# Loading the cached values in runs of eight pages instead of one page after each key page

## The chip, the cores and the metric

The kernel runs on one core of one Trainium2 chip. The metric is the device time of one launch in microseconds (us). Three runs of the kernel before took 4829.04, 4834.27 and 4845.87 us, so its median is 4834.27 us.

The core has a matrix engine (PE; its weight loads are listed as PEld), a vector engine (DVE), a scalar engine (ACT), a general engine (POOL) and a queue engine (SP) that here does nothing but wait for semaphores and issue DMA transfers, strictly in the order of its program.

## The reference

One inference step of a decoder with two layers. Each layer projects 2048 prompt tokens and 8 x 4 sample tokens, runs an RWKV-7 recurrence over one half of the width and differential attention over the other, and projects back. The part that this change touches is the attention:

```python
def diff_attend(q, k, v, q_pos, k_pos, lam):
    s = jnp.einsum('bqhcd,bkhcd->bhcqk', q, k) / math.sqrt(DIFF_HEAD_DIM)
    s = jnp.where(k_pos[None, :] <= q_pos[:, None], s, -jnp.inf)
    p = jax.nn.softmax(s, axis=-1)
    attn = p[:, :, 0] - lam * p[:, :, 1]
    return jnp.einsum('bhqk,bkhe->bqhe', attn, v)

def diff_sample(q, k, v, lam, k_pool, v_pool, page_table):
    k_past = k_pool[page_table].reshape(B, -1, DIFF_HEADS, 2, DIFF_HEAD_DIM)
    v_past = v_pool[page_table].reshape(B, -1, DIFF_HEADS, DIFF_V_DIM)
    k_all = jnp.concatenate([k_past, k], axis=1)
    v_all = jnp.concatenate([v_past, v], axis=1)
    return diff_attend(q, k_all, v_all, past + jnp.arange(T), jnp.arange(past + T), lam)
```

The prompt has 4 heads of 2048 positions. Each of the 8 sample sequences has 2048 cached positions, kept in 16 pages of 128 positions (for all 4 heads together a page of keys is 256 KB, and a page of values as well). Where a page lies in HBM is read from the page table at run time.

## The kernel before

A loop runs the two layers. Each layer has five stages with a barrier between them: input projection, RWKV, attention, the RWKV part of the samples, output projection. The change is in the attention stage, `attn_sync` and its helpers, all of it code for the SP queue.

**The prompt's attention.** It goes over tiles t = 0 to 63, sixteen for each of four heads h, each tile being 128 query rows of a head. PE makes the scores of tile t in blocks j of 512 keys (`scores`, L1354), DVE copies them out of PSUM, ACT takes the exponentials (L1158), DVE combines the two maps, PE turns the result of tile t-2 (`turn_map`, L1370), ACT copies it out (L1167) and PE multiplies it with the values (`values`, L1382). Queries and keys of a head, which the code calls its maps, are two transfers of 1 MB each into one of two buffers `kq[h % 2]` (`load_map`, L985). The head's values come by a third transfer of 1 MB (`load_values`, L1006).

**The samples' attention rides along.** The table `BESIDE` lists 200 places (t, j) between blocks of the prompt's work. Sequence b owns 31 of them, and they start at place 24 b; its piece number k is done at place 24 b + k. In `beside_tensor`:

- pieces 1 to 16 turn key pages 0 to 15 with four transposes each (L1118) and then signal `t_made`;
- pieces 9, 11, 14 and 17 make the scores of four pages each (L1110);
- pieces 21 to 24 turn the probabilities (L1127);
- pieces 22, 23, 26 and 27 multiply with value groups 0 to 3, four pages each (L1138), and signal `pv_done`.

A sequence with odd b = 2 h + 1 is turned in tiles 16 h + 9 to 16 h + 13. PE runs its program in order: a transpose that waits for its page holds up everything behind it, the prompt's work too.

**Buffers and what the SP queue waits for.** Key pages go through KS = 4 buffers, so page p of a sequence can be asked for when page p - 4 has been turned (the wait in `keys_sync`). Value pages go through two buffers of four pages. Group n, counted over all sequences (n = 4 b + g), waits until group n - 2 has been multiplied. The maps of head h + 1 wait until head h has begun. All of these are issued by SP, one after the other.

**The order on the SP queue before.** For each sequence b: key page 4, value page 0, key page 5, value page 1, and so on to key page 11 and value page 7; then key pages 12 to 15. For odd b below 7 the first map of the next head stands behind key page 12 and the second behind key page 14, and the next head's values stand behind key page 15. Then come key pages 0 to 3 of the next sequence and, last, value pages 8 to 15 in a row.

On the ACT queue a gate transfer of 1 MB is issued at tile 16 h + 10 (L1189).

Of the kernel before, what the change touches and what calls it, by code (L numbers as in the profile page):

```python
# [39 lines left out]
HEADS = 4  # L40
# [5 lines left out]
Q_ROW, K_ROW, V_ROW, DG_ROW = 2176, 2688, 3200, 3712  # L46
NEG = -1e30
N_PHYS = 160
# [66 lines left out]
def build(nc, ins, outs):  # L115
# [4 lines left out]
    with ctx:  # L120
        def sb(name, shape, dt=F32):
            return ctx.enter_context(nc.sbuf_tensor(name, shape, dt))
# [4 lines left out]
        def sem(name):  # L127
            return ctx.enter_context(nc.semaphore(name))
# [140 lines left out]
        def rwkv_sync(sp, l):  # L269
# [7 lines left out]
            for s in SLOTS:  # L277
                u, t, n, q, r, m, lt = roles(s)
                if lt is not None:
                    if lt:  # L280
                        lV.wait(sp, lt - 1, 1)
                    in_lora.inc(sp.dma_start(rawl[:, :], PT[bass.ds(l * COLS + 3 * RW, P), lt * TQ:lt * TQ + TQ + 1]))
                    in_lora.close()
                if m is not None:
                    if m:
                        pV.wait(sp, m - 1, sV_XV)
                    for j in (1, 0, 2):
                        in_raw.inc(sp.dma_start(raw[:, j, :, :], rows(j * RW + m % 2 * 2 * P, 2 * P, 2, m // 2 * TQ, TQ + 1)))
                    in_raw.close()
                if q is not None:  # L290
                    if q:
                        fV.wait(sp, q - 1, F_SG)
                    in_gate.inc(sp.dma_start(gate[:, :, :], rows(GATE_ROW, RW, 4, q * P + 1, P)))
                    in_gate.close()
                if s == NU - 1:
                    attn_ahead(sp, l)
                if r is not None:
                    fW.wait(sp, r, F_MIX)
                    stored.inc(sp.dma_start(MT[0:RW, r * P:(r + 1) * P].rearrange("(c p) t -> p c t", c=4), mix[:, r % 2, :, :]))
                    stored.close()  # L300
# [573 lines left out]
        PG, NP, KS, NSEQ = 128, SEQ // 128, 4, 8  # L874
# [16 lines left out]
        kq = (kq0, kq1)  # L891
# [4 lines left out]
        vpg, PTs, vt_s, Pn, u_st = cv(8, 512), cv(2, 4, P), cv(512), cv(NS), cv(16)  # L896
        ident_b, dmask_b = sb("ident_b", [P, P], BF16), sb("dmask_b", [P, P], BF16)
        osq_s, ors, omx = [Pq[:, i * P:(i + 1) * P].rearrange("p (c t) -> p c t", c=4) for i in range(3)]
        ptab = sb("ptab", [1, 8 * NP], I32)
        c_sems = []  # L900

        def csem(name):
            c_sems.append(psem("c_" + name))
            return c_sems[-1]
        c_v, c_g, c_lam, c_lv, mask_ok = [csem(n) for n in ("in_v", "in_gate", "lam", "lv", "mask")]
        c_kq, c_cst, u_in, c_sto = [sem(n) for n in ("c_in_kq", "c_cst", "u_in", "c_store")]
# [5 lines left out]
        u_k, u_v = [csem(f"page_k{i}") for i in range(KS)], [csem(f"page_v{i}") for i in range(2)]  # L912
        u_lv, u_q, vt_made, vt_out, u_sto = [csem(n) for n in ("u_chain", "queries", "vt_made", "vt_out", "u_store")]
        scored, s_out, max_ok, exp_ok, coef_ok = [csem(n) for n in ("u_scores", "u_scores_out", "u_max", "u_exp", "u_coef")]
        pn_turned, pn_out, pv_done, o_out, o_folded, o_kept = [csem(n) for n in ("pn_turned", "pn_out", "pv", "u_o_out", "o_folded", "o_kept")]
# [42 lines left out]
        def t_full(eng, *use):  # L958
            eng.wait_ge(t_made, USE[use] + 1)
# [4 lines left out]
        def keys_sync(sp, l, b, ps):  # L964
            for p in ps:
                q = b * NP + p
                if q >= KS:
                    t_full(sp, "k", (q - KS) // NP, (q - KS) % NP)
                pg = sp.value_load(ptab[0:1, q:q + 1], min_val=0, max_val=N_PHYS - 1)
                sp.dma_start(kpg[:, q % KS, :], ins["cache_k"][bass.ds(l * N_PHYS + pg, 1)].rearrange("n p c -> (n p) c")).then_inc(u_k[q % KS], 16)  # L970

        def value_sync(sp, l, b, q):
            n = b * 4 + q // 4
            if n >= 2 and q % 4 == 0:
                sp.wait_ge(pv_done, n - 1)
            pg = sp.value_load(ptab[0:1, b * NP + q:b * NP + q + 1], min_val=0, max_val=N_PHYS - 1)
            sp.dma_start(vpg[:, n % 2 * 4 + q % 4, :], ins["cache_v"][bass.ds(l * N_PHYS + pg, 1)].rearrange("n p c -> (n p) c")).then_inc(u_v[n % 2], 16)

        def map_rows(l, h, r):
            return PT[bass.ds(l * COLS + h * P + r, P), 1:SEQ + 1]  # L980

        def load_map(sp, l, h, i):
            if h and i == 0:
                sp.wait_ge(s_ok, first(NT * (h - 1)) + 1)
            sp.dma_start(kq[h % 2][:, i, :], map_rows(l, h, (Q_ROW, K_ROW)[i])).then_inc(c_kq, 16)  # L985

        def attn_ahead(sp, l):
            pV.wait(sp, NU - 1, sV_BV)
            pA.wait(sp, NU - 1, sA_SQ)
            pT.wait(sp, NU - 1, sT_BO)  # L990
            for i in range(2):
                load_map(sp, l, 0, i)
            sp.dma_start(dmask[:, :], ins["dmask"]).then_inc(c_cst, 16)
            sp.dma_start(lam[:, :, :], ins["lam"][bass.ds(l, 1)].rearrange("l p a b -> (l p) a b")).then_inc(c_cst, 16)
            sp.dma_start(sub[:, 0:3], ins["sub"][bass.ds(l, 1)].rearrange("l p a -> (l p) a")).then_inc(c_cst, 16)
            sp.dma_start(ptab[:, :], ins["ptab"]).then_inc(u_in, 16)
            for dst, src in ((qT_s, Q_ROW), (kT_s, K_ROW), (vT_s, V_ROW), (g_s, DG_ROW)):
                sp.dma_start(dst[:, :, :], PT[bass.ds(l * COLS + src, 512), SEQ + 1:].rearrange("(h p) t -> p h t", p=P)).then_inc(u_in, 16)
            for dst, src in ((n_m, "nmask"), (fold, "fold"), (u_cs, "csel"), (onesP, "ones")):
                sp.dma_start(dst, ins[src]).then_inc(u_in, 16)  # L1000

        def attn_sync(sp, l):
            def load_values(h):
                if h:
                    t_full(sp, "v", h - 1, 3)
                sp.dma_start(vT[:, :], map_rows(l, h, V_ROW)).then_inc(c_v, 16)  # L1006

            load_values(0)
            sp.wait_ge(u_in, U_IN)
            keys_sync(sp, l, 0, range(KS))  # L1010
            for b in range(NSEQ):
                h = b // 2
                ahead = b % 2 and h + 1 < HEADS
                for p in range(KS, NP):
                    keys_sync(sp, l, b, (p,))
                    if p < KS + 8:
                        value_sync(sp, l, b, p - KS)
                    if ahead and p in (12, 14):
                        load_map(sp, l, h + 1, (p - 12) // 2)
                if ahead:  # L1020
                    load_values(h + 1)
                if b + 1 < NSEQ:
                    keys_sync(sp, l, b + 1, range(KS))
                for q in range(8, NP):
                    value_sync(sp, l, b, q)

        def beside_scalar(act, b, k):
            if K_AT <= k < K_AT + NP:
# [859 lines left out]
        @block.sync  # L1888
        def _(sp):
            sp.dma_start(ones[:, :], ins["ones"]).then_inc(c_one, 16)  # L1890
            for g in range(NG):
                sp.dma_start(XN[:, :, cols(g)], kgt(x_in, g)).then_inc(n_x[g], 16)
            sp.dma_start(ident[:, :], ins["ident"]).then_inc(c_ld, 16)
            sp.dma_start(fw[:, :], ins["fw"]).then_inc(c_ld, 16)
            sp.wait_ge(n_ssq, NG)
            sp.dma_start(xcur, x_in).then_inc(c_x, 16)
            with sp.Fori(0, DEPTH) as l:
                proj_sync(sp, l)
                ph.end(sp, l, 0, leader=True)
                rwkv_sync(sp, l)  # L1900
                ph.end(sp, l, 1, leader=True)
                attn_sync(sp, l)
                rsmp_ahead(sp, l)
                ph.end(sp, l, 2, leader=True)
                sp.dma_start(wo[:, :, :], ins["w_out"][bass.ds(l, 1)].rearrange("l p k n -> (l p) k n")).then_inc(d_cst, 16)
                ph.end(sp, l, 3, leader=True)
                out_sync(sp, l)
                ph.end(sp, l, 4, leader=True)
            for g in range(NG):
                sp.wait_ge(y_v, 6 * (g + 1))  # L1910
                sp.wait_ge(y_p, 2 * (g + 1))
                sp.dma_start(kgt(outs["y"], g), yb[:, :, cols(g)]).then_inc(y_st, 16)
            sp.wait_ge(y_st, 16 * NG)
# [174 lines left out]
```

## Time and profile before

| | |
|---|---|
| runs | 4829.04, 4834.27, 4845.87 us |
| the profiled execution's own time | 4845.87 us |
| its span, first to last instruction | 4844.0 us |
| mean granted PE clock | 0.925 of full speed |
| PE busy | 4082.8 us, 84% |
| DVE, ACT, POOL busy | 42%, 36%, 10% |
| DMA, mean over the span | 88 GB/s |

The profile covers one execution. Its page gives, for each engine, the time it was busy, and the chain of work that ended last. From the trace behind the page come timelines of one engine, tables by stretch with busy time and granted clock, and for any DMA the time from issue to landing. A timeline row gives start and duration in us, the engine (with a q for its sequencer), the source line, the operation, what it writes and reads, how many instructions were merged, and in brackets how long the engine was idle before it and who ended that. Names: `in_cache_k` and `in_cache_v` are the key and value pages, `out_proj_t` holds the projections, from which maps and values of the prompt are read, and `arena` is the on-chip memory.

### The profile page before, as it was taken

The page shows a single profiled execution, that of the slowest core. Times are in us where ns is not written, and L with a number is a line of the kernel's source. Part 1 is how long each engine was busy: PE and PEld are TensorE (multiplying, and loading weights), DVE is VectorE, ACT ScalarE, POOL GpSimd, SP SyncE. Part 2 cuts the span into 40 slices and gives each one's busy share as a digit, 9 for nine tenths or more (in the row PEclk, how much of TensorE's full clock was granted, in tenths as well). Part 3 has the DMA queues.
Part 4 walks back from the last instruction along what each step waited for, and adds up shares of the span by engine and source line. Part 5 has one row for each costly group of instructions (what it writes and reads, how often), then busy time and mean ns, then how long its engine had stood idle before and what let it go on. Part 6 is the DMA issues. An engine that isn't in the chain of part 4 may idle for free.

```text
span 4844.0 us, 114299 instructions
## 1 busy us (share of the span) xinstructions
PE 4082.8 (84%) x49138; PEld 3547.0 (73%) x49138; DVE 2024.8 (42%) x4536; ACT 1751.0 (36%) x3584; POOL 482.7 (10%) x264
## 2 busy tenths in 40 slices
PE   3999999688787888877989999978788688888595
PEld 2999999577674565556989999967777555565495
DVE  3211111566655555553231111136666455555335
ACT  3000000566655666541110000026666565666211
POOL 1322221000000000010032222200000000000201
PEclk9999999799998999987989999979999899999597
DMA  4211111111113454243221111111111243453333
GB/s 164 79 66 75 71 66 58 55 35 47 37 44 89 159 162 138 90 143 123 95 73 73 66 75 71 58 64 38 37 40 32 76 144 113 137 166 101 128 116 127
DMA packets 227651, 427.63 MB, mean 88 GB/s; under 512 B 32162, under 2 KB 137636, under 8 KB 212900
## 3 DMA queue, kind: packets, MB, share of 16 engines
q1 hardware_dynamic: 212164, 330.79, 21.4%
q10 hardware_dynamic: 14976, 89.46, 4.6%
q8 instruction: 390, 6.39, 0.6%
q14 instruction: 121, 0.99, 0.1%
HBM read 304.91 MB, written 123.80 MB: 89 GB/s over the span
## 4 chain that ended last, share of the span: by engine, by line
PE 70%; DVE 12%; ACT 9%; issue 4%; DMA 2%; SPq 2%; POOL 1%; ACTq 0%; DVEq 0%
PE psum L1883 10%; PE psum L1884 10%; PE psum L1885 10%; PE psum L1354 4%; PE psum L1382 4%; PE psum L703 3%; PE psum L1528 3%; PE psum L1530 3%; PE psum L1529 2%; PE psum L1370 2%; PE psum L1118 2%; ACT arena L1158 2%; PE psum L700 2%; PE psum L774 1%; PE psum L1110 1%
## 5 line engine op out<-in xcount | busy, mean ns | idle before, releaser
L1883 PE MATMUL psum<-x_hi,w_parts 128*128 128x416 f32 x2640 | 931.9, 353 | 59.8 <-POOL w_parts L1841 59.8
L1884 PE MATMUL psum<-x_lo,w_parts 128*128 128x416 f32 x2640 | 927.8, 351 | 0.0
L1885 PE MATMUL psum<-x_hi,w_parts 128*128 128x416 f32 x2640 | 927.6, 351 | 0.0
L1850 DVE TENSOR_TENSOR arena<-psum,arena 128x416 f32<-128x416 f32 x330 | 195.6, 593 | 1284.4 <-PE psum L1885 1284.2
L322 ACT ACTIVATE arena<-arena 128x256 f32<-128x256 f32 x16 | 8.2, 514 | 1544.4 <-DVE arena L446 1544.4
L1883 PEld LDWEIGHTS psum<-x_hi,w_parts 128*128 128x128 f32 x2640 | 497.2, 188 | 67.6 <-POOL w_parts L1841 63.2
L1885 PEld LDWEIGHTS psum<-x_hi,w_parts 128*128 128x128 f32 x2640 | 497.5, 188 | 6.5
L1884 PEld LDWEIGHTS psum<-x_lo,w_parts 128*128 128x128 f32 x2640 | 498.7, 189 | 4.5
L1261 DVE TENSOR_SCALAR_CACHE_REDUCE arena<-psum 128x512 f32<-128x512 f32 (+3 forms) x640 | 357.5, 608 | 294.5 <-PE psum L1354 154.7
L1382 PE MATMUL psum<-arena 128*128 128x128 f32 x2176 | 311.1, 285 | 64.0 <-ACT arena L1167 46.8
L1354 PE MATMUL psum<-arena 64*128 64x512 f32 (+3 forms) x1280 | 329.1, 618 | 41.1 <-DVE arena L1261 22.4
L1382 PEld LDWEIGHTS psum<-arena 128*128 128x128 f32 x2176 | 278.8, 199 | 78.3 <-issue 51.4
L1158 ACT ACTIVATE arena<-arena 128x128 f32<-128x128 f32 (+15 forms) x256 | 309.0, 1207 | 8.2 <-DVE arena L1267 8.2
L1528 PE MATMUL psum<-m_hi,wo_hi 128*128 128x416 f32 x640 | 229.4, 358 | 40.7 <-DVE m_lo L1499 40.7
L1707 POOL MEMSET arena<- 128x32 f32 x2 | 0.3, 157 | 2614.9 <-SPq L107 2614.9
L1167 ACT ACTIVATE arena<-psum 128x512 f32<-128x512 f32 (+3 forms) x320 | 170.3, 532 | 248.5 <-PE psum L1370 248.5
L1838 POOL TENSOR_TENSOR w_parts<-arena 128x1024 fp32r<-128x1024 f32 (+1 forms) x68 | 126.8, 1864 | 1305.2 <-PE psum L1885 980.3
L1370 PE MATMUL psum<-ident,arena 128*128 128x128 f32 x1088 | 189.5, 292 | 64.8 <-DVE arena L1274 40.7
L1370 PEld LDWEIGHTS psum<-ident,arena 128*128 128x128 f32 x1088 | 123.6, 147 | 161.7 <-DVE arena L1274 67.2
L1530 PE MATMUL psum<-m_hi,wo_lo 128*128 128x416 f32 x640 | 226.6, 354 | 0.0
L1034 ACT ACTIVATE arena<-psum 128x512 f32<-128x512 f32 x256 | 154.9, 605 | 197.7 <-PE psum L1118 197.6
L703 PE MATMUL psum<-arena 64*64 64x64 f32 x5120 | 193.5, 227 | 37.7 <-DVE arena L508 26.5
(339 smaller groups left out, 6764.6 us busy)
## 6 DMA issues: line engine op xcount, KB each, us to landing
out_proj_t<-arena ACTq DMA_DIRECT2D x66, 1040.5 KB, 4.1
arena<-in_cache_k SPq DMA_DIRECT2D x256, 256.0 KB, 2.8
arena<-in_cache_v SPq DMA_DIRECT2D x256, 256.0 KB, 3.0
arena<-in_w_in SPq DMA_DIRECT2D x66, 512.0 KB, 3.5
arena<-out_proj_t SPq DMA_DIRECT2D x96, 257.0 KB, 3.1
arena<-out_proj_t SPq DMA_DIRECT2D x24, 1024.0 KB, 5.7
m_raw<-mixed_t SPq DMA_DIRECT2D x10, 1664.0 KB, 7.3
x_res<-x_cur SPq DMA_DIRECT2D x10, 1664.0 KB, 18.0
```

The source lines that it names most:

```text
L703: mm = pe.matmul(b8(2)[at(h, j), ix(c, h), :], Yp[at(h, j), ix(c, h), :], XT[at(h, j), u % 2, ix(c, h), :], start=True, stop=True)
L1158: e = act.activation(src, src, ACT.Exp, bias=nm[:, t % 2, a:a + 1], accum_out=l12[:, par(t), i, a:a + 1])
L1261: x_ = dve.tensor_scalar(dst, bank[2 * (J % 2) + a][:, 0:w], 0.125, NEG, ALU.mult, ALU.max, accum_out=mxp[:, t % 2, a, j:j + 1])
L1354: mm = pe.matmul(bank[2 * (J % 2) + a][:, 0:w], kq[h % 2][hs(a), 0, i * P:(i + 1) * P], kq[h % 2][hs(a), 1, j * GRP:j * GRP + w], start=Tr ...
L1370: mm = pe.transpose(bank[4][:, c * P:(c + 1) * P], S0[:, t % 3, k * P:(k + 1) * P], ident[:, :])
L1382: mm = pe.matmul(bank[5][:, 0:P], PT_[:, G % 4, c, :], vtok[:, k, :], start=(k == 0), stop=(k == i))
L1528: pe.matmul(bank[q % 3][:, 0:TG], wh, mh, start=(k == 0), stop=False)
L1530: mm = pe.matmul(bank[q % 3][:, 0:TG], wl, mh, start=False, stop=(k == KT - 1))
L1850: dve.tensor_tensor(ost[:, b % 2, 1 + g * TG:1 + (g + 1) * TG], bank[q % 8][:, 0:TG], RSTD[:, cols(g)], ALU.mult).then_inc(p_ev, 1)
L1883: pe.matmul(bank[q % 8][:, 0:TG], w_hi[:, b % 3, k, :], x_hi[:, k, cols(g)], start=(k == 0), stop=False)
L1884: pe.matmul(bank[q % 8][:, 0:TG], w_hi[:, b % 3, k, :], x_lo[:, k, cols(g)], start=False, stop=False)
L1885: mm = pe.matmul(bank[q % 8][:, 0:TG], w_lo[:, b % 3, k, :], x_hi[:, k, cols(g)], start=False, stop=(k == KT - 1))
```

## The change

The change reorders what SP issues in the attention stage. The transfers, their number, sizes, buffers and semaphores stay, and no other engine's program is changed. For each sequence b the order is now: key pages 4 to 7; value pages 0 to 7; for odd b below 7 both maps of the next head; key pages 8 to 15; the next head's values; key pages 0 to 3 of the next sequence; value pages 8 to 15.

```diff
-        def value_sync(sp, l, b, q):
-            n = b * 4 + q // 4
-            if n >= 2 and q % 4 == 0:
-                sp.wait_ge(pv_done, n - 1)
-            pg = sp.value_load(ptab[0:1, b * NP + q:b * NP + q + 1], min_val=0, max_val=N_PHYS - 1)
-            sp.dma_start(vpg[:, n % 2 * 4 + q % 4, :], ins["cache_v"][bass.ds(l * N_PHYS + pg, 1)].rearrange("n p c -> (n p) c")).then_inc(u_v[n % 2], 16)
+        def values_sync(sp, l, b, gs):
+            for g in gs:
+                n = b * 4 + g
+                if n >= 2:
+                    sp.wait_ge(pv_done, n - 1)
+                for p in range(4 * g, 4 * g + 4):
+                    pg = sp.value_load(ptab[0:1, b * NP + p:b * NP + p + 1], min_val=0, max_val=N_PHYS - 1)
+                    sp.dma_start(vpg[:, n % 2 * 4 + p % 4, :], ins["cache_v"][bass.ds(l * N_PHYS + pg, 1)].rearrange("n p c -> (n p) c")).then_inc(u_v[n % 2], 16)
...
-        def load_map(sp, l, h, i):
-            if h and i == 0:
+        def load_maps(sp, l, h):
+            if h:
                 sp.wait_ge(s_ok, first(NT * (h - 1)) + 1)
-            sp.dma_start(kq[h % 2][:, i, :], map_rows(l, h, (Q_ROW, K_ROW)[i])).then_inc(c_kq, 16)
+            for i, r in enumerate((Q_ROW, K_ROW)):
+                sp.dma_start(kq[h % 2][:, i, :], map_rows(l, h, r)).then_inc(c_kq, 16)
...
             for b in range(NSEQ):
                 h = b // 2
-                ahead = b % 2 and h + 1 < HEADS
-                for p in range(KS, NP):
-                    keys_sync(sp, l, b, (p,))
-                    if p < KS + 8:
-                        value_sync(sp, l, b, p - KS)
-                    if ahead and p in (12, 14):
-                        load_map(sp, l, h + 1, (p - 12) // 2)
-                if ahead:
+                keys_sync(sp, l, b, range(KS, 8))
+                values_sync(sp, l, b, (0, 1))
+                if b % 2 and h + 1 < HEADS:
+                    load_maps(sp, l, h + 1)
+                keys_sync(sp, l, b, range(8, NP))
+                if b % 2 and h + 1 < HEADS:
                     load_values(h + 1)
                 if b + 1 < NSEQ:
                     keys_sync(sp, l, b + 1, range(KS))
-                for q in range(8, NP):
-                    value_sync(sp, l, b, q)
+                values_sync(sp, l, b, (2, 3))
```

The first place is on SP in sequence b = 1, from the issue of key page 7 to that of key page 8. A page is four instructions: a load of its number from the table, arithmetic on it, and the DMA (L969 and L970 for keys, L976 and L977 for values). `phase_sem21` is `t_made`, the signal of a turned page. Before:

```order
L969 TENSOR_LOAD ptab [waits phase_sem21]
L969 ISA x2
L970 ISA
L970 DMA arena<-in_cache_k 128x512
L976 TENSOR_LOAD ptab
L976 ISA x2
L977 ISA
L977 DMA arena<-in_cache_v 128x512
L969 TENSOR_LOAD ptab [waits phase_sem21]
L969 ISA x2
L970 ISA
L970 DMA arena<-in_cache_k 128x512
```

One value page stood between two key pages. Now, at the same place ahead of key page 8 (values at L978 and L979, maps at L988, `phase_sem5` is `s_ok`), beginning with the last of the eight value pages:

```order
L978 TENSOR_LOAD ptab
L978 ISA x2
L979 ISA
L979 DMA arena<-in_cache_v 128x512
L988 ISA [waits phase_sem5]
L988 DMA arena<-out_proj_t 128x2048
L988 ISA
L988 DMA arena<-out_proj_t 128x2048
L969 TENSOR_LOAD ptab [waits phase_sem21]
L969 ISA x2
L970 ISA
L970 DMA arena<-in_cache_k 128x512
```

Between key pages 7 and 8 there are now eight value pages and both maps, where one value page was. In even sequences and in b = 7 there are the eight value pages alone.

The second place is on SP where the second map used to be, in b = 1, behind key page 14 (L1006 is the next head's values). Before:

```order
L985 ISA
L985 DMA arena<-out_proj_t 128x2048
L969 TENSOR_LOAD ptab [waits phase_sem21]
L969 ISA x2
L970 ISA
L970 DMA arena<-in_cache_k 128x512
L1006 ISA [waits phase_sem21]
L1006 DMA arena<-out_proj_t 128x2048
```

Now key page 15 stands ahead of the values without a map before it:

```order
L970 DMA arena<-in_cache_k 128x512
L1008 ISA [waits phase_sem21]
L1008 DMA arena<-out_proj_t 128x2048
L969 TENSOR_LOAD ptab [waits phase_sem21]
L969 ISA x2
```

What follows from there, four key pages of the next sequence and eight value pages, stands in the order it had.

## Rows read from the trace of the kernel before

**Rows 1.** The page: the chain that ended last, by engine.
```profile
PE 70%; DVE 12%; ACT 9%; issue 4%; DMA 2%; SPq 2%; POOL 1%; ACTq 0%; DVEq 0%
```
**Rows 2.** Stretches (us, busy by engine, clock, DMA share, GB/s): one attention stage; four tiles.
```profile
1480.00:2140.00 660.00, 558.60 (x4608) 377.42 (x4606) 374.23 (x1162) 401.08 (x892) 0.00 (x0) 0.93 0.42 134
...
1738.00:1778.00 40.00, 37.74 (x341) 26.04 (x339) 22.96 (x71) 27.55 (x63) 0.00 (x0) 1.00 0.81 274
```
**Rows 3.** PE's waits for pages: values (us, times, longest); keys (us, times).
```profile
PE psum L1138 <- DMA arena<-in_cache_v: 9.2, 7, 1.8
...
  DMA arena<-in_cache_k: 1.5, 1
```
**Rows 4.** Timeline of PE, sequence 3 of layer 0: key pages 3, 8, 9, 12.
```profile
1745.44 0.60 PE L1118 MATMUL psum<-ident,arena 128*128 128x128 f32 x4
...
1758.67 0.66 PE L1118 MATMUL psum<-ident,arena 128*128 128x128 f32 x4
...
1760.11 0.63 PE L1118 MATMUL psum<-ident,arena 128*128 128x128 f32 x4
...
1767.68 0.63 PE L1118 MATMUL psum<-ident,arena 128*128 128x128 f32 x4
```
**Rows 5.** Timeline of SP, from key page 12 of that sequence on.
```profile
1760.09 0.33 SPq L970 DMA_DIRECT2D arena<-in_cache_k  x1
1760.62 0.33 SPq L985 DMA_DIRECT2D arena<-out_proj_t  x1
...
1765.98 0.33 SPq L985 DMA_DIRECT2D arena<-out_proj_t  x1
...
1767.62 0.33 SPq L1006 DMA_DIRECT2D arena<-out_proj_t  x1
1769.07 8.71 SPq L970 DMA_DIRECT2D arena<-in_cache_k  x4
```
**Rows 6.** SP: eight value pages in a row; two maps in a row.
```profile
1792.74 8.04 SPq L977 DMA_DIRECT2D arena<-in_cache_v  x8
...
1427.55 0.90 SPq L985 DMA_DIRECT2D arena<-out_proj_t  x2
```
**Rows 7.** Landing, key page issued at 1765.4 with nothing large ahead.
```profile
DMA to landing us min/median/max: 2.7/2.7/2.7
```
**Rows 8.** Landing, key pages behind two large transfers, issued at 1769.1 and 1608.0.
```profile
DMA to landing us min/median/max: 7.5/7.5/7.5
...
DMA to landing us min/median/max: 6.1/6.1/6.1
```
**Rows 9.** Landing, the two maps issued at 1427.55; the values issued from 1792.74.
```profile
DMA to landing us min/median/max: 6.2/7.2/8.2
...
DMA to landing us min/median/max: 2.5/2.9/3.5
```
**Rows 10.** PE, key pages 3 and 8: sequences 7 and 0, layer 0; 5, layer 1.
```profile
2069.63 0.60 PE L1118 MATMUL psum<-ident,arena 128*128 128x128 f32 x4
...
2082.86 0.66 PE L1118 MATMUL psum<-ident,arena 128*128 128x128 f32 x4
...
1518.55 0.60 PE L1118 MATMUL psum<-ident,arena 128*128 128x128 f32 x4
...
1533.12 1.12 PE L1118 MATMUL psum<-ident,arena 128*128 128x128 f32 x4
...
4277.33 0.60 PE L1118 MATMUL psum<-ident,arena 128*128 128x128 f32 x4
...
4290.56 0.66 PE L1118 MATMUL psum<-ident,arena 128*128 128x128 f32 x4
```
**Rows 11.** Stretches around an idle PE, columns as in rows 2.
```profile
1656.00:1658.00 2.00, 0.00 (x0) 0.00 (x0) 1.16 (x7) 2.00 (x4) 0.00 (x0) 0.95 0.82 247
1658.00:1664.00 6.00, 5.60 (x16) 2.77 (x17) 3.56 (x6) 3.63 (x9) 0.00 (x0) 0.50 0.24 64
...
1825.00:1828.40 3.40, 3.40 (x13) 1.57 (x11) 2.32 (x8) 1.68 (x4) 0.00 (x0) 0.51 0.00 0
```

More of the change, by code:

```diff
@@ L990, in attn_ahead @@
             pT.wait(sp, NU - 1, sT_BO)
-            for i in range(2):
-                load_map(sp, l, 0, i)
+            load_maps(sp, l, 0)
             sp.dma_start(dmask[:, :], ins["dmask"]).then_inc(c_cst, 16)
```

## The prediction, made before the changed kernel ran

> **What bounds the kernel now.** I read the page's chain of waits first: 70% of it is PE [rows 1], so the kernel goes as fast as PE can be kept going. The change is in the attention stage alone, so next I read the stretches. Each of the two attention stages has about 660 us, of which PE is busy 558.6; around the odd sequences it is busy 37.7 us of 40 at full clock, with DVE at 23 and ACT at 28 [rows 2]. There PE is the bound, and an idle PE is lost time. Then PE's waits for pages: in the whole run 9.2 us for values (7 times) and 1.5 us for keys (once) [rows 3]. All that a better order of the page loads can win is therefore 10.7 us; what it can lose has no such lid. Last come the timelines of PE and SP side by side, which give the distances used below.
>
> **What the change moves.** Nothing is added or removed: 256 key pages, 256 value pages, 16 maps and 8 prompt values are issued as before, and all engines but SP run the same program. What counts is how late each transfer lands against its first use. I go through the moved pieces.
>
> *Key page 8 in sequences 1, 3 and 5.* SP can issue key page 7 when page 3 has been turned. I take sequence 3 of layer 0. The turning of page 3 ends at 1745.44 + 0.60 = 1746.04, and that of page 8 begins at 1758.67, which is 12.63 later [rows 4]. The same distance stands in sequence 5 of layer 1: 4277.33 + 0.60 to 4290.56 is 12.63 [rows 10]. The new queue then runs like this, counted from the end of the turning of page 3:
> - from a turned page to the issue of the key page that waited for it: page 12 of this sequence is turned at 1767.68 + 0.63 = 1768.31 [rows 4] and the waiting load is issued at 1769.07 [rows 5], so 0.76. Key page 7 goes out at 0.76.
> - eight value pages: eight in a row take 8.04 us, the last of them 0.33, so 7.71 / 7 = 1.10 each [rows 6]. The last goes out at 0.76 + 8.8 = 9.56. Both signals that they need are there: the groups of the sequence before are multiplied at pieces 26 and 27, which are this sequence's pieces 2 and 3, and at the same place the older sequence comes first.
> - first map: 0.53 behind a page (1760.09 to 1760.62 [rows 5]), so at 10.09; second map 0.90 - 0.35 = 0.55 later [rows 6], at 10.64. The signal that the maps wait for comes at tile 16 h, some nine tiles earlier.
> - key page 8: a page costs 1.10, so it goes out at 11.74. PE wants it at 12.63, that is 0.89 later.
>
> A key page with nothing large ahead lands 2.7 us after its issue [rows 7]. This one has 2 MB ahead of it. The nearest rows are the first key pages of the next sequence, which stand behind a map and the prompt's values (2 MB and a page, spread over 3.1 us of issue): they land 7.5 and 6.1 us after issue [rows 8]. The pair of maps at the stage's start lands 6.2 and 8.2 us after issue [rows 9]. The second of them, at 10.64 + 8.2 = 18.8, would put the key page at 7.1 after its own issue at the earliest. I take 7.4, near the upper row, because the maps are now issued closer together. Key page 8 lands at 11.74 + 7.4 = 19.1 and PE stands for 19.1 - 12.6 = 6.5 us. Ends for this term: 2.7 gives 1.8 us, 6.1 gives 5.2 us, and 8.0 gives 7.1 us.
>
> The Trainium skill ("DMA: Bandwidth & Descriptors", Anatomy of one DMA) gives about 2.0 us and the bytes at 436 GB/s for one transfer, fitted on another path than this queue's. As an estimate, two maps and a page are 2.36 MB, which is 5.4 + 2.0 = 7.4 us after the first map; the key page would land at 17.5, the stall would be 4.9 us and the sum below 9.6 us smaller. The pair of maps took 0.55 + 8.2 = 8.75 us without the page [rows 6, 9], so the rows say that the page is somewhat too fast here, and I stay with the rows.
>
> There are six such places: sequences 1, 3 and 5 in two layers. 6 x 6.5 = 39 us.
>
> *Behind that stall.* Key pages 9, 10 and 11 go out 1.1 us apart and are wanted from 1.4 us after page 8 on (1758.67 to 1760.11 [rows 4]); they land behind it a page at a time and add nothing. Page 12 waits for page 8 to be turned and is wanted 9.0 us after it (1767.68 - 1758.67 [rows 4]), against 0.66 + 0.76 + 2.7 = 4.1 needed. The lag ends there.
>
> *Clock.* After PE has been idle the granted clock drops from 2.4 to 1.2 GHz for a while: PE does nothing from 1656 to 1658, and 1658 to 1664 runs at 0.50; a shorter pause leads to 3.4 us at 0.51 [rows 11]. In a stretch where PE is the bound half of such a time is lost, between 1.7 and 3.0 us, or nothing where it falls into the idle time itself. A pause of 6.5 us is longer than these. I take 1.7, since the drop can begin before PE resumes. 6 x 1.7 = 10 us.
>
> *What is won back.* While PE stands, ACT and DVE finish what they have, so that PE's short waits behind it shrink. PE has 40 - 37.7 = 2.3 us of them in 40 us here, and more further on (660 - 558.6 = 101 us in a stage) [rows 2]. Most of those are a round trip through ACT and DVE that starts from PE's own work and moves with it, so I take 1.5, with ends 0 and the whole stall. 6 x 1.5 = 9 us back.
>
> *Key page 8 in sequence 7* has no maps ahead: issued at 9.56 + 1.10 = 10.66, landed at 13.4, wanted at 2082.86 - 2070.23 = 12.63 [rows 10]. 0.8 us, twice: 1.6 us. Ends 0 and 2.
>
> *Key page 8 in even sequences.* In sequence 0 it is wanted at 1533.12 - 1519.15 = 13.97 [rows 10], and lands at 13.4: hidden with 0.6 to spare. In sequences 2, 4 and 6 the prompt's tiles with few blocks leave longer distances still. Cost 0; if that small cover is gone, about 1 us each.
>
> *Everything else.* Value pages 0 to 7 are wanted at piece 22, some 45 us on in an odd sequence, and the eight land 2.5 to 3.5 us after issue even in a row [rows 9]: hidden. Key pages 4 to 7 lose the value pages between them and go out up to 2 us sooner, but PE does not wait for them now, so no gain. The maps come earlier than they did and are wanted at tile 16 (h + 1). Value pages 8 to 15, on which the 9.2 us of waits rest [rows 3], keep their place: no gain, no loss.
>
> **Sum.** 39 + 10 - 9 + 1.6 = 42 us on the profiled execution's own 4845.9 us (span 4844.0), so 4888. That execution was the slowest of the three; from the median of 4834.3 it is 4876.
>
> **Rivals.**
> - *The key page does not queue behind the maps* but shares the DMA engines with them and lands after 2.7 us. The stall is 1.8 us, 6 x 1.8 + 1.6 = 12 us, 4847. For it: pages behind other pages land in 2.5 to 3.5 us [rows 9]. Against it: 6.1 and 7.5 behind large ones [rows 8].
> - *The stall is absorbed*, the rival that ends not slower. PE is idle 101 us in a stage anyway [rows 2]. If its waits behind each stall shrink by more than 6.5 us, because ACT and DVE had been late by their own backlog, the six stalls cost nothing and the time is 4834 + 2 = 4836. It decides from the point at which ACT, not PE, sets the pace. Against it: ACT is busy 28 us of 40 here and has little backlog to give back.
> - *The order gains.* All page waits go: 10.7 us [rows 3], 4824. It would need the maps not to matter and the value waits to end, whose transfers did not move.
> - *Slow clock after every stall.* 7.1 us of stall, 3.0 us of clock, nothing won back: 6 x 10.1 + 2 = 63 us, 4897.
>
> **How the numbers follow.** A difference of about 0.3% (14.5 us) is what a measurement of this kernel can tell from none. Chances: forecast 0.67 (its own range 4856 to 4890), slow clock 0.13, sharing 0.09, absorbed 0.06, gain 0.05. The predicted time is 4876. The range reaches from sharing to slow clock, 4845 to 4897. Forecast and slow clock are slower by over 0.3%: 0.80. Sharing and absorbed are within it, and so is most of gain: 0.18. Faster by more: 0.02.
>
> **What would show it.** In the changed kernel's profile PE's waits at L1118 for key pages rise from 1.5 us to about 40 us, in six waits of 5 to 8 us, each at the turning of key page 8 of sequences 1, 3 and 5, with SP having issued two maps just before that page and its landing 6 to 8 us after issue; two small waits stand in sequence 7. The clock falls to half just behind each. The attention stages grow by about 20 us each, and no other stage changes. I am wrong if the key page lands within 4 us of its issue, if PE's idle time behind the stalls shrinks by as much as they take, or if the value groups 2 and 3 no longer make PE wait.

## The result and the profile after

The changed kernel takes 4905.82 us (median of four runs, 4891.27 to 4907.05) against 4837.76 us for the kernel before, run beside it. The ratio is 1.0134 with a 95% interval of 1.0107 to 1.0162: slower, as forecast, but by 68 us where 42 were forecast, and above the upper end of the range (4897). The profiled execution took 4906.05 us, which is 60.2 us more than the profiled one of before.

First where the time went. Stretches of the changed kernel, columns as in [rows 2]: the two attention stages, from the first to the last PE instruction.

```profile
1500.40:2186.90 686.50, 566.53 (x4606) 385.04 (x4606) 373.30 (x1161) 399.46 (x888) 0.00 (x0) 0.92 0.41 128
3889.70:4567.30 677.60, 562.10 (x4606) 380.88 (x4606) 372.45 (x1159) 399.33 (x888) 0.00 (x0) 0.92 0.42 129
```

And of the kernel before, the same two stages:

```profile
1489.70:2139.20 649.50, 558.28 (x4606) 377.40 (x4606) 372.05 (x1159) 399.54 (x888) 0.00 (x0) 0.93 0.43 135
3855.80:4508.50 652.70, 561.96 (x4606) 381.99 (x4606) 372.98 (x1160) 399.58 (x888) 0.00 (x0) 0.93 0.43 134
```

They grew by 37.0 and 24.9 us, 62 us together, and that is the whole difference of the two spans (60.2 us). DVE and ACT have the same busy time. (The attention stage of layer 0 also starts 10.7 us later, but the RWKV stage of layer 1 is 11.7 us shorter: those stages, which the change does not touch, vary so from run to run.)

Next the waits of PE's matmuls in the changed kernel (total us, times, longest), against [rows 3]:

```profile
PE psum L1117 <- DMA arena<-in_cache_k: 50.6, 9, 8.6
PE psum L1381 <- ACT arena L1166: 46.7, 48, 1.9
PE psum L1137 <- DMA arena<-in_cache_v: 11.3, 9, 2.1
```

Before, no matmul waited for a key page. The 1.5 us of [rows 3] is the wait of one weight load (PEld), which the view by line puts together with PE's; this sum went from 1.5 to 115.0 us, of which 50.6 are the matmuls' own. The wait for values is 2.1 us longer than the 9.2 us of before; in the other eight traces it is 7.5 to 10.5 us. The middle row matters below: before, PE waited for the same copies on ACT like this,

```profile
PE psum L1382 <- ACT arena L1167: 46.8, 48, 1.9
```

so these short waits gave nothing back. Nor did the others: by the stretches above, PE's idle time in the two stages (length less busy time) grew from 182.0 to 235.5 us, that is by 53.5 us, 2.9 us more than the waits for key pages.

One of the stalls close up. PE's timeline of the changed kernel, sequence 3 of layer 0 (L1117 is the turning of a key page, the first row is page 3, then 7, 8 and 9), against [rows 4]:

```profile
1765.36 0.60 PE L1117 MATMUL psum<-ident,arena 128*128 128x128 f32 x4
...
1775.73 0.60 PE L1117 MATMUL psum<-ident,arena 128*128 128x128 f32 x4
...
1786.65 1.11 PE L1117 MATMUL psum<-ident,arena 128*128 128x128 f32 x4 [8.00 <-DMA arena<-in_cache_k]
1787.56 1.92 PE L1381 MATMUL psum<-arena 128*128 128x128 f32 x8
1789.27 1.06 PE L1117 MATMUL psum<-ident,arena 128*128 128x128 f32 x4
```

SP's timeline there (key page 7, eight value pages, two maps, key page 8 and more), against [rows 5, 6], and below it the landing of key page 8, in us after its issue:

```profile
1766.73 0.33 SPq L970 DMA_DIRECT2D arena<-in_cache_k  x1
1768.15 8.92 SPq L979 DMA_DIRECT2D arena<-in_cache_v  x8
1777.28 0.87 SPq L988 DMA_DIRECT2D arena<-out_proj_t  x2
1778.94 9.91 SPq L970 DMA_DIRECT2D arena<-in_cache_k  x5
...
DMA to landing us min/median/max: 7.7/7.7/7.7
```

The two maps ahead of it, issued from 1777.28:

```profile
DMA to landing us min/median/max: 6.2/7.2/8.1
```

Counted from the end of the turning of page 3 (1765.96), key page 8 goes out at 12.98 where 11.74 was forecast, lands at 20.65 and stalls PE for 8.00 us. The second map lands at 19.97, so the page lands 0.7 us behind it. It is so at every place where a map stands just ahead of key page 8: in the 24 places of four kernels (this one, and r2_maps_only, r6_gate_early and r8_one_map below) the page lands 0.6 to 0.7 us behind the last map. That is the queueing that the forecast assumed.

Then the four matmuls of a turning and the eight of L1381 take 1.11 and 1.92 us; L1381 took 1.06 us ahead of the stall. That is the clock. Stretches of the changed kernel, the stall and what follows, columns as before:

```profile
1778.70:1786.60 7.90, 0.00 (x0) 0.00 (x0) 0.70 (x2) 0.00 (x0) 0.00 (x0) 0.83 0.97 374
1784.00:1790.70 6.70, 4.05 (x18) 3.72 (x20) 0.00 (x0) 0.94 (x2) 0.00 (x0) 0.50 0.63 225
1790.80:1797.00 6.20, 5.34 (x41) 3.09 (x37) 2.93 (x12) 5.59 (x13) 0.00 (x0) 1.00 0.22 62
```

In the stall PE, DVE and ACT do next to nothing while the transfers run at 374 GB/s. The granted clock is 0.50 (1.2 GHz) from 1784.0 to 1790.7, so four microseconds of it lie behind the stall. The Trainium skill ("TensorE: Matmul & The Clock Gate", Part 1) says that the throttled state is the default and activity releases it; this trace agrees, with 0.50 in the later part of 8 us without a matmul and 1.00 again from 1790.8.

What the slow clock costs can be read from the distances between turnings. From the turning of key page 8 to that of page 12 it is 9.0 us before and 10.4 to 11.8 us behind the six stalls. From page 12 to page 15, and on to the first page of the next sequence, every distance is that of before to 0.1 us: the whole delay is still there.

All nine waits for key pages in the changed kernel, place by place:

| place | issue of page 8 after page 3 | landing | stall |
|---|---|---|---|
| layer 0, sequence 1 / 3 / 5 | 12.1 / 13.0 / 12.0 | 8.0 / 7.7 / 9.2 | 7.5 / 8.0 / 8.5 |
| layer 1, sequence 1 / 3 / 5 | 12.1 / 12.6 / 11.8 | 8.0 / 8.7 / 7.1 | 7.5 / 8.6 / 6.3 |
| sequence 7, layer 0 / 1 | 10.7 / 10.7 | 5.0 / 2.9 | 3.0 / 1.0 and 0.3 |
| even sequences | 10.6 to 11.0 | 2.9 to 3.6 | none |

### The profile page after: what moved, and what is told of

Its sections match the earlier page's. It is cut to its first block, busy times and chain, and to the rows that moved or that the text cites. A ratio compares the mean times of both kernels' runs of the same rounds, so it can differ in the third digit from the quotient of the medians.

```text
span 4904.2 us, 114299 instructions
## 1 busy us (share of the span) xinstructions
PE 4100.2 (84%) x49138; PEld 3565.4 (73%) x49138; DVE 2023.0 (41%) x4536; ACT 1750.1 (36%) x3584; POOL 480.8 (10%) x264
## 4 chain that ended last, share of the span: by engine, by line
PE 68%; DVE 12%; ACT 8%; issue 4%; DMA 4%; SPq 3%; POOL 1%; ACTq 0%; DVEq 0%
PE psum L1882 10%; PE psum L1883 10%; PE psum L1884 10%; PE psum L1353 4%; PE psum L1381 3%; PE psum L703 3%; PE psum L1527 3%; PE psum L1529 3%; PE psum L1528 2%; PE psum L1369 2%; PE psum L1117 2%; PE psum L700 2%; ACT arena L1157 2%; PE psum L774 1%; DVE arena L508 1%
## 5 line engine op out<-in xcount | busy, mean ns | idle before, releaser
L1381 PE MATMUL psum<-arena 128*128 128x128 f32 x2176 | 314.2, 287 | 63.9 <-ACT arena L1166 46.7
L1381 PEld LDWEIGHTS psum<-arena 128*128 128x128 f32 x2176 | 281.6, 200 | 78.3 <-issue 51.4
L1528 PE MATMUL psum<-m_lo,wo_hi 128*128 128x416 f32 x640 | 225.6, 353 | 0.0
```

Of the source, the lines that this page charges most:

```text
L1381: mm = pe.matmul(bank[5][:, 0:P], PT_[:, G % 4, c, :], vtok[:, k, :], start=(k == 0), stop=(k == i))
L1528: pe.matmul(bank[q % 3][:, 0:TG], wh, ml, start=False, stop=False)
```

## The experiments

The theory after the result: key page 8 is late because SP issues eight value pages and two maps ahead of it and because it then queues behind 2 MB of maps; the stall comes back in full and brings slow clock with it; the short waits give nothing back. Eight kernels were run. The table has, for each, the sum of the waits of PE's matmuls for key pages (0 before), the growth of the two attention stages over the 1302.1 us of before (both from the profile), and the growth of the median over the kernel before on the same chip. A median's difference is uncertain by 5 to 13 us, as the intervals show.

| kernel | waits for keys | stages | median | ratio, 95% interval |
|---|---|---|---|---|
| changed | 50.6 | +62.0 | +68.1 | 1.0134, 1.0107 to 1.0162 |
| r1_values_only | 15.2 | +9.7 | +10.9 | 1.0023, 1.0010 to 1.0036 |
| r2_maps_only | 7.1 | -1.9 | +6.8 | 1.0007, 0.9992 to 1.0022 |
| r3_maps_first | 30.7 | +42.4 | +36.9 | 1.0073, 1.0057 to 1.0090 |
| r4_wait_only | 43.6 | +54.8 | +58.1 | 1.0116, 1.0099 to 1.0134 |
| r5_maps_even | 0 | -6.7 | +4.6 | 1.0009, 0.9998 to 1.0020 |
| r6_gate_early | 50.6 | +54.6 | +58.8 | 1.0130, 1.0108 to 1.0152 |
| r7_wait_short | 27.2 | +29.6 | +40.0 | 1.0083, 1.0063 to 1.0102 |
| r8_one_map | 38.2 | +43.0 | +48.0 | 1.0102, 1.0083 to 1.0122 |

**r1_values_only**, one half of the change (the helper `load_map`, put back for it, is left out here):

```diff
                 values_sync(sp, l, b, (0, 1))
-                if b % 2 and h + 1 < HEADS:
-                    load_maps(sp, l, h + 1)
-                keys_sync(sp, l, b, range(8, NP))
+                keys_sync(sp, l, b, range(8, 13))
+                if b % 2 and h + 1 < HEADS:
+                    load_map(sp, l, h + 1, 0)
+                keys_sync(sp, l, b, range(13, 15))
+                if b % 2 and h + 1 < HEADS:
+                    load_map(sp, l, h + 1, 1)
+                keys_sync(sp, l, b, range(15, NP))
```

> Half of the change: value pages 0 to 7 in a run ahead of key page 8, but both maps back behind key pages 12 and 14. Theory (the stall is the sum of eight page issues and the landing behind 2 MB of maps): in all eight odd sequences key page 8 goes out 10.7 us after the turning of page 3, lands 3 to 5 us later and PE stands 1 to 3 us, as the changed kernel shows in sequence 7 (3.0 and 1.2 us). 8 x 2 = 16 us and a little clock, so about 18 us over before, near 4856. Rival (the run of values is what costs, wherever the maps are): stalls of 5 us and more in all odd sequences, 35 us or more over before.

Eight places with stalls of 1.1 to 3.1 us, 15.2 us in all, and +10.9 us where 18 were expected (the interval is 4.8 to 17.4). The account of the stalls holds, the rival is out. That the time grew by less than the stalls is within what the interval allows.

**r2_maps_only**, the other half:

```diff
                 for p in range(KS, NP):
+                    if ahead and p == 8:
+                        load_map(sp, l, h + 1, 0)
+                        load_map(sp, l, h + 1, 1)
                     keys_sync(sp, l, b, (p,))
...
-                    if ahead and p in (12, 14):
-                        load_map(sp, l, h + 1, (p - 12) // 2)
```

> The other half: values one by one between the keys as before, but both maps just ahead of key page 8 in sequences 1, 3 and 5. Theory: key page 8 goes out 4.0 + 1.1 = 5.1 us after the turning of page 3 and lands 7 to 9 us later, at 12.1 to 14.1, against 12.63 wanted: stalls of 0 to 1.5 us, 0 to 10 us in all, near 4843. Rival (maps ahead of a wanted key page cost their transfer time wherever SP stands): six stalls of 6 to 8 us, 40 us or more.

Key page 8 went out at 4.6 to 5.3 us and landed 8.4 to 9.5 us later: six stalls of 0.4 to 2.0 us, and no difference in time that can be told from none. Each half alone costs 7 to 15 us of stalls, both together 50.6. The margin explains this by itself. In the kernel before, key page 8 of the odd sequences landed 4.2 to 5.4 us ahead of its use. The run of values makes it land 5 to 8 us later, the two maps 5 to 7 us later, both together 10 to 13 us later, and only what exceeds the margin is a stall.

**r3_maps_first**, the order of the two runs swapped:

```diff
-                values_sync(sp, l, b, (0, 1))
                 if b % 2 and h + 1 < HEADS:
                     load_maps(sp, l, h + 1)
+                values_sync(sp, l, b, (0, 1))
```

> The changed kernel with both maps ahead of the run of eight value pages instead of behind it; the same transfers stand ahead of key page 8. Theory: it goes out 11.9 us after the turning of page 3, as before, but most of the maps have moved by then; it lands in 3 to 5 us, stalls of 2.5 to 5 us, about 33 us over before in all, near 4870. Rival A (only the number of bytes ahead counts): as slow as the changed kernel, 62 us over. Rival B (SP's issue time alone counts): landing in 2.7 us, stalls of 2 us, 15 us over.

Key page 8 went out at 12.2 to 12.7 us and landed 4.2 to 5.3 us later; the stalls are 4.2 to 4.8 us. The second map had landed 0.6 to 2.6 us before the page went out. Both rivals are out: neither the bytes alone nor SP's time alone decides, but SP's time plus what the transfers have not yet moved when the page goes out. The wait is in this trace like this (total, times, longest):

```profile
PE psum L1117 <- DMA arena<-in_cache_k: 30.7, 11, 4.8
```

**r4_wait_only**, a stall without the burst:

```diff
                 for p in range(KS, NP):
+                    if ahead and p == 8:
+                        for _ in range(25):
+                            sp.value_load(ptab[0:1, 0:1], min_val=0, max_val=N_PHYS - 1)
                     keys_sync(sp, l, b, (p,))
```

> The kernel before, with 25 loads of a page number into a register, unused, ahead of key page 8 in sequences 1, 3 and 5. They keep SP busy for some 13 us with no transfer. Key page 8 goes out at about 17 us after the turning of page 3 and lands in 2.8 us: a stall of some 7 us, as in the changed kernel, without the burst of transfers. It prices a stall by itself. Theory now (a stall comes back in full and brings 1.9 us of slow clock): the attention stages grow by 1.25 times the summed stalls, about 50 us, near 4890. The recorded term (1.5 us won back at each) would make it 1.0 times the stalls. Rival (the burst of transfers, not the stall, costs a part): clearly less than the stalls.

This is the run that tests the recorded term of 1.5 us won back at each stall, and it refutes it. Its waits, and the stretches during and behind the stall of sequence 3, columns as above:

```profile
PE psum L1121 <- DMA arena<-in_cache_k: 43.6, 6, 7.6
```

```profile
1781.00:1788.60 7.60, 0.43 (x4) 0.00 (x0) 0.70 (x2) 0.00 (x0) 0.00 (x0) 0.67 0.15 40
1788.70:1796.00 7.30, 7.29 (x38) 4.93 (x38) 1.64 (x5) 3.54 (x8) 0.00 (x0) 0.65 0.80 243
```

With 40 GB/s in the stall there is no burst, and the loss is of the same kind: 43.6 us of stalls, 54.8 us of stage time, 58.1 us of median. A stall costs 1.26 times itself here and 62.0 / 50.6 = 1.23 times itself in the changed kernel. On the spot the same is seen: from page 8 to page 12 it takes 1.8 to 2.4 us longer than before, 12.8 us at the six places, and from there to the next sequence's first page nothing is made up. DVE and ACT stand too (0.70 us and nothing in 7.6): they had no backlog to work off.

**r7_wait_short**, the same with fewer loads:

```diff
-                        for _ in range(25):
+                        for _ in range(18):
```

> The kernel before with 18 instead of 25 unused loads ahead of key page 8: it goes out at 13.6 us, lands at 16.3, six stalls of 3.7 us with no burst of transfers, 22 us in sum. If long stalls bring slow clock and short ones do not, the time rises by the stalls or less, near 4858; if every stall costs 1.3 times itself, by 29 us, near 4867.

The stalls are 3.2 to 3.9 us, but page 9 then waits as well in four sequences, up to 1.3 us, since it is issued two transfers later, and pages 13 and 15 wait up to 0.8 us; 27.2 us in all where I expected 22. The median grows by 40 us, the stages by 29.6 us. Stalls of 3 us and more do bring slow clock: in four of the six places the granted clock stood at half behind the stall. Shorter ones mostly do not: in r2_maps_only five of the six stalls, 0.4 to 1.9 us, left the distance from page 8 to page 12 at 9.0 us, and one of 2.0 us made it 1.6 us longer. My first case is out; how the factor runs with the length of the stall stays open, since stages and median differ by 10 us here.

**r6_gate_early**, whether the gate's transfer explains the longer landing:

```diff
-                if s_ == 10 and t < NTILE:
+                if s_ == 9 and t < NTILE:
                     load_gate(h)
```

> The changed kernel with the gate's transfer of 1 MB (ACT queue) at tile 16h + 9 instead of 16h + 10, some 5 us sooner. It stands for what my sum left out: in the changed kernel key page 8 went out 12.1 to 13.0 us after the turning of page 3 instead of 11.74 and landed 7.1 to 9.2 us later instead of 7.4. If the gate is the cause of both, the six stalls fall from 7.7 to about 6.5 us and those of sequence 7 from 3.0 and 1.2 to 0.8, 12 us faster than the changed kernel, near 4893. If it is not, stalls and time stay, 4906.

A miss. Page 8 went out at the same 11.8 to 12.7 us and landed 7.0 to 9.8 us later, with the same 50.6 us of waits. In sequence 7 the waits were 3.1 us in sum instead of 4.2. Against its own kernel before the median is 58.8 us up where the changed kernel's is 68.1, but the ratios' intervals overlap and the waits did not move, so I make nothing of it; that 4893 us is the very figure of the case that failed is luck. The gate is not what makes the page land late behind the maps. The traces say why: in the changed kernel the gate had landed 2.3 to 3.0 us after the turning of page 3, at least 7.7 us before key page 8 went out. The edit moved its issue by some 15 us, not 5.

**r8_one_map**, one map ahead instead of two:

```diff
                 values_sync(sp, l, b, (0, 1))
                 if b % 2 and h + 1 < HEADS:
-                    load_maps(sp, l, h + 1)
-                keys_sync(sp, l, b, range(8, NP))
+                    load_map(sp, l, h + 1, 0)
+                keys_sync(sp, l, b, range(8, 15))
+                if b % 2 and h + 1 < HEADS:
+                    load_map(sp, l, h + 1, 1)
+                keys_sync(sp, l, b, range(15, NP))
```

> The changed kernel with only the first map ahead of key page 8, the second back behind key page 14. Theory (each map ahead adds its bytes, 2.6 us, and 0.54 us of issue): key page 8 goes out at 11.6 us and lands 5.4 us later, six stalls of 4.4 us, with sequence 7 about 30 us, near 4873. Rival (either map is enough to hold the page up fully): stalls of 7 us, 4900.

Key page 8 went out at 11.2 to 12.2 us as expected but landed 5.8 to 7.2 us later, not 5.4: stalls of 5.2 to 6.2 us, and 4882 us, between the two cases. So without a map it lands in about 3.0 us (r1), behind one in 6.7 (mean of six), behind two in 8.1. The first map costs more than the second. A sum of map bytes over one rate does not give these numbers.

**r5_maps_even**, the version that the experiments point to, the maps where key pages have 20 us to spare:

```diff
                 ahead = b % 2 and h + 1 < HEADS
+                early = b % 2 == 0 and h + 1 < HEADS
...
-                    if ahead and p in (12, 14):
+                    if early and p in (12, 14):
```

> The kernel before, with both maps of the next head behind key pages 12 and 14 of the even sequence 2h instead of the odd one 2h + 1, where the key pages have 20 us to spare. Theory: the maps stood where they cost nothing already (no wait of PE for key pages in the odd sequences before), so nothing changes, within 3 us of before. Rival (the traffic of the odd sequences slows the pages that PE does wait for, values 8 to 15): up to 10 us faster.

As before, no matmul waits for a key page and one weight load waits 1.5 us, and the time does not differ from before (1.0009, 0.9998 to 1.0020). The order of before already hid its maps; none of these versions beats it.

## Why the prediction was wrong

The stalls came where they were forecast: page 8 of sequences 1, 3 and 5, a small one in sequence 7, none in the even ones, half clock behind each of the six. The cost was not as forecast. On the profiled executions' attention stages, where the sum was made:

- **Stalls of sequences 1, 3 and 5: 39 forecast, 46.4 measured.** The page went out 12.3 us after the turning of page 3 on average instead of 11.74. Part of it can be seen in the timeline above: the eight value pages took 8.92 us there instead of 8.04, because one of their DMA instructions took 1.22 us where the others took 0.33; why is open. And it landed after 8.1 us instead of 7.4: the second map landed 8.55 us after its issue, where 8.2 was taken, and the page 0.7 us behind it, where 0.3 was allowed. The upper end of that term, 7.1 us, lies below the mean stall of 7.7.
- **Won back: -9 forecast, 0 measured.** This is the step that failed, and the largest error. I argued against myself in one paragraph (the short waits are round trips that move with PE's work, "so I take 1.5") and took a value between where the argument gave 0. The waits of 46.8 us for ACT's copies stayed at 46.7, the distances between the turnings behind each stall did not shrink, and r4_wait_only shows both with nothing but a stall. The 101 us that the forecast read as short waits in a stage were also too many: the stretch of [rows 2] began 10 us ahead of the stage, whose own idle time is 91 us.
- **Clock: 10 forecast, 13 measured**, as the longer way from key page 8 to page 12: 11.7 us at the six places and 1.7 us in sequence 7.
- **Sequence 7: 1.6 forecast, 4.2 measured.** In layer 0 its page landed after 5.0 us with no map ahead. The 2.7 us of [rows 7] was a low value: in the kernel before, key page 8 of the odd sequences landed after 3.1 to 5.0 us. Why it varies is open: in the four kernels with the run of values and the gate in its place it landed in sequence 7 after 2.8 to 5.1 us, and with the gate sooner after 2.7 and 3.4.
- **Sum: 42 forecast.** The four come to 64; the stages grew by 62 and the medians by 68. For the execution that it was made on the sum gave 4888 us, and 4906 were measured.

No single error takes the time out of the range; together they do, and the base adds some. The profiled execution of before, 4845.9 us, was the slowest of its first three, and the traces show one reason. Ahead of each odd sequence PE has several short waits, the last of 1.9 us for ACT. In that execution the clock fell to half twice there, 13.7 us apart and for 3.4 us each, at seven of the eight such places: once well ahead of the wait of 1.9 us (in the place below behind waits of 1.3, 1.5 and 0.7 us) and again right behind it. In the changed kernel's it did so at four, in the other eight traces at one to eight. In the 80 places of the ten traces both falls came together 40 times, neither 39 times, and the second alone once. Where both came, the next key page came 2.9 us later. The two stretches ahead of sequence 5 of layer 0 before, and the second of them after (columns as above):

```profile
1876.30:1879.70 3.40, 3.40 (x16) 2.53 (x12) 2.52 (x7) 0.60 (x1) 0.00 (x0) 0.50 0.00 0
...
1888.90:1893.30 4.40, 4.40 (x46) 3.26 (x48) 2.27 (x3) 3.72 (x9) 0.00 (x0) 0.61 0.01 4
```

```profile
1921.00:1925.40 4.40, 4.40 (x52) 2.80 (x52) 2.19 (x3) 3.80 (x9) 0.00 (x0) 1.00 0.03 8
```

Three such pairs fewer take 9 us off the changed kernel's stages, so the 64 us come to 55 against 62 measured. Of the 7 us between, the longer waits for values are 2.1 us, and behind the longest of them (2.15 us, at the start of sequence 4 of layer 0) the clock fell to half for 6.8 us where it had not before, 2.9 us; 2 us are not accounted for. My sum was made on one execution and moved to the median as it stood.

The rivals: sharing is out (pages landed in 7 to 9 us), absorbed and gain are out. The slow-clock case, at 4897, had the missing recovery right and its stall of 7.1 us was nearer to the 7.7 measured; with 0.13 it was given too little.

## What to carry to other kernels

A queue that issues in order gives a page a lead, here four buffers, 12.6 us from the release of one to the need of another; sum what is issued ahead of it (1.1 us a page, 0.55 us a map) and what is still to land, and compare with the lead: each half of this change nearly fits and both do not. Where PE is the bound and its short waits are round trips through other engines, count a stall of 3 us and more in full and add a sixth to a half for the clock (medians grew by 1.16 to 1.47 times the waits in the six kernels with waits over 20 us; r1_values_only and r2_maps_only, with mostly shorter stalls, grew by 0.7 and 1.0 times, within intervals too wide to tell); take something off only for an engine that is seen to have a backlog. Put large transfers where the lead is longest, not beside a run of small ones.

## What the runs showed of the hardware

- A 256 KB page behind two 1 MB transfers of the same queue lands after 7.0 to 9.8 us (18 places in the changed kernel, r2_maps_only and r6_gate_early), behind one after 5.8 to 7.2 us, behind pages alone mostly in 3 us and at most 5.4 us (key page 8 in all ten traces). Behind maps it lands 0.6 to 0.7 us after the last of them (24 places).
- In the changed kernel key page 8 of sequences 1, 3 and 5 went out 0.0 to 1.2 us later than the sum of single issues said: in five of the six places one or two issues in the run of values took 1.4 to 2.0 us instead of 1.1. Why is open.
- 25 unused loads of a number from on-chip memory on SP, each with its arithmetic and range check, took 13.6 to 14.0 us, 0.55 us each.
- After the same short waits of PE, the longest 1.9 us, the granted clock falls to half in some executions and not in others (at one to eight of eight places), twice for 3.4 us, at 2.9 us for the two. Two profiled executions that differ by less than 20 us should be compared by their waits before they are compared by their spans.
